# The state stage of an RWKV branch on one NeuronCore: diagonal blocks gathered from PSUM under a mask ahead of the masked copies, the output tail deferred by a tile, and the PSUM banks dealt anew

## The reference

```
for each token t:
    S = S * decay_t                       # per key channel
    sa = S . kk_t                         # what the state holds for this key
    S = S - outer(sa, b_t) + outer(v_t, k_t)
    y_t = S . r_t
out = (group_norm(y) * g + b + bonus_t * v_t) * gate_t
```

## Time and profile before

| | us |
|---|---|
| median of 3 runs | 5111.66 (5102.7 to 5111.89) |
| the profiled execution | 5108.83 |
| its span | 5107.0 |
| window 1835 to 2760, which holds the state stage | 925.0 |
| mean granted clock of the whole span | 0.907 |

### The profile page before, as it was taken

One profiled execution on the slowest core, in us unless ns is written; L12 is line 12 of the kernel. 1 busy time (PEld: TensorE's weight loads), 2 busy tenths in 40 slices (PEclk: granted clock), 3 DMA queues, 4 the chain that ended last, 5 costly groups with the idle time before them and its releaser, 6 DMA issues. The chain is left out here.

```text
span 5107.0 us, 67890 instructions
## 1 busy us (share of the span) xinstructions
PE 4415.9 (86%) x24875; PEld 3721.9 (73%) x24932; DVE 2559.9 (50%) x4995; ACT 1321.3 (26%) x2626; POOL 598.2 (12%) x585
## 2 busy tenths in 40 slices
PE   8999688887799958888886999799979799699869
PEld 6777577776577748878885888677868577577657
DVE  4444334444566655554553434577753333467733
ACT  3222222111222211111111111566641211222211
POOL 0000011111000012222221111000000011011100
PEclk9999799999899967777776999799989899899979
DMA  3111311111543321100102222610023422422233
GB/s 132 58 53 50 123 56 56 56 64 38 184 137 129 122 77 38 33 32 29 37 31 89 99 111 103 185 41 28 15 75 133 146 103 97 148 87 89 81 122 115
DMA packets 218306, 434.06 MB, mean 85 GB/s; under 512 B 36547, under 2 KB 90436, under 8 KB 218022
## 3 DMA queue, kind: packets, MB, share of 16 engines
q1 hardware_dynamic: 218150, 432.02, 24.8%
HBM read 248.33 MB, written 146.93 MB: 77 GB/s over the span
## 5 line engine op out<-in xcount | busy, mean ns | idle before, releaser
L235 PE MATMUL rp_pj<-rp_w_high,rp_hT_high 128*128 128x512 f32 (+1 forms) x640 | 239.5, 383 | 27.2 <-DVE rp_w_low L178 14.4
L235 PE MATMUL fp_pj<-fp_w_high,fp_hT_high 128*128 128x512 f32 (+2 forms) x640 | 220.7, 359 | 43.8 <-DVE fp_w_low L178 43.8
L2484 DVE TENSOR_SCALAR_CACHE_REDUCE fa_sm<-fa_sc 128x512 f32<-128x512 f32 (+2 forms) x320 | 194.4, 610 | 93.3 <-PE fa_sc L2325 82.9
L236 PE MATMUL rp_pj<-rp_w_low,rp_hT_high 128*128 128x512 f32 (+1 forms) x640 | 233.6, 374 | 0.0
L235 PE MATMUL hg_pj<-hg_w_high,hg_hT_high 128*128 128x512 f32 x512 | 210.1, 410 | 17.1 <-DVE hg_w_low L178 17.1
L235 PE MATMUL rc_pj<-rc_w_high,rc_hT_high 128*128 128x512 f32 (+1 forms) x512 | 192.6, 384 | 34.5 <-DVE rc_w_low L178 34.4
L236 PE MATMUL fp_pj<-fp_w_low,fp_hT_high 128*128 128x512 f32 (+2 forms) x640 | 219.2, 357 | 0.0
L1527 PE MATMUL rw_b<-rw_U_parts_high,rw_pick_row 128*128 128x128 f32 x256 | 106.4, 416 | 116.3 <-DVE rw_U_parts_low L178 116.3
L236 PE MATMUL hg_pj<-hg_w_low,hg_hT_high 128*128 128x512 f32 x512 | 205.1, 400 | 0.0
L2339 PE MATMUL fa_tp<-fa_ident,fa_sm 128*128 128x128 f32 x1088 | 175.1, 282 | 31.4 <-DVE fa_pT_low L178 14.8
L2432 ACT CAST fa_pT_high<-fa_tp 128x512 fp32r<-128x512 f32 (+1 forms) x288 | 160.9, 559 | 147.5 <-PE fa_tp L2339 145.3
(11 more groups left out here) (552 smaller groups left out, 11634.2 us busy)
## 6 DMA issues: line engine op xcount, KB each, us to landing
rw_given<-rw_packed_dram SPq DMA_DIRECT2D x48, 512.0 KB, 4.2
rc_back<-rc_XB SPq DMA_DIRECT2D x48, 336.0 KB
rw_packed_dram<-rp_M SPq DMA_DIRECT2D x48, 256.0 KB, 2.6
rp_M<-rp_U SPq DMA_DIRECT2D x16, 728.0 KB, 4.8
hg_xt<-in_x SPq DMA_DIRECT2D x16, 512.0 KB, 3.7
kept_x_high_dram<-hg_hT_high SPq DMA_DIRECT2D x16, 512.0 KB, 3.5
kept_x_low_dram<-hg_hT_low SPq DMA_DIRECT2D x16, 512.0 KB, 4.3
sw_hT_high<-kept_x_high_dram SPq DMA_DIRECT2D x16, 512.0 KB, 3.7
```

Of the source, the lines that this page charges most:

```text
L235: pe.matmul(out, hT.high[:, kc, :], self.high[:, kc, lo:hi], start=kc == 0, stop=False)
L236: pe.matmul(out, hT.high[:, kc, :], self.low[:, kc, lo:hi], start=False, stop=False)
L2484: dve.tensor_scalar(sm[:, to:to + cols], bank_of(slot)[:, 0:cols], 0.0, NEG, ALU.add, ALU.max, accum_out=tops[:, four, c:c + 1]).then_inc( ...
```

## The change

Five things change, all in `rwkv`:
1. `compact_blocks` no longer reads `BA` from SBUF with four operations over 32 partitions each. It multiplies the four PSUM products with a mask `near` (own 16x16 block, above the diagonal) into `X`, sums the eight blocks with one reduction into `Uc`, and comes ahead of all masked copies.
2. The spread is cut in two halves on other banks (6, 7, then 2, 3), and the last group of products (n = 1, r = 1) goes between the halves, into banks 0 and 1, after the first two copies of `BA`.
3. The solve waits for six masked copies instead of eight; the read-out waits for all eight. Banks: Z 4, y 5, state product 1. The wait for the renewed state moves from the transposes to level 4.
4. The third part of `finish` becomes `put_out` and is done one tile later, after the state is renewed; `y`, `gain` and `rest` get a second buffer, and the store follows a step later. Parts 0 and 1 stand ahead of levels 5 and 6, which is where they stood.
5. POOL makes the two corners of level 4 first, each behind its two copies of `BA`, and `gain` and `rest` after them. The decay of the state on DVE moves behind the masked copies of `BA` and two of `KA`.

```diff
-        Y_BANK, Z_BANK, INC_BANK = 5, 6, 7
+        Z_BANK, Y_BANK, INC_BANK = 4, 5, 1
+        SPREAD = (6, 7, 2, 3)
-        PRODUCT_BANKS = (((0, 1), (2, 3)), ((4, 5), (6, 7)))
+        PRODUCT_BANKS = (((0, 1), (2, 3)), ((4, 5), (0, 1)))
...
@@ PE
-                    for n in range(2):
-                        for r in range(2):
-                            multiply(i, pi, n, r)
-                    spread(i)
+                    multiply(i, pi, 0, 0)
+                    multiply(i, pi, 0, 1)
+                    multiply(i, pi, 1, 0)
+                    spread(i, 0)
+                    pe.wait_ge(masked, 8 * i + 2)
+                    multiply(i, pi, 1, 1)
+                    pe.wait_ge(masked, 8 * i + 4)
+                    spread(i, 1)
                 if m:
                     if pr:
-                        pe.wait_ge(masked, 8 * i + 8)
+                        pe.wait_ge(masked, 8 * i + 6)
                     solve(t, pt)
-                    read_out(t, pt)
+                    read_out(t, pt, i)
...
@@ DVE
-            def compact_blocks(i, pi):
-
+            def compact_blocks(i):
+
+                for r in range(2):
+                    dve.wait_ge(products, 4 * i + r + 1)
+                    for o in range(2):
+                        tt(X[:, 4 * r + o:4 * r + 4:2, :], heads(B[PRODUCT_BANKS[0][r][o]][:], 2)[:, :, 0:P], again(near[:], 2), ALU.mult)
+                dve.drain()
+                dve.tensor_reduce(Uc[:], X[:].rearrange("p h (b t) -> p h t b", t=SMALL), AX, ALU.add)
+                dve.drain()
+                dve.tensor_copy(Up.high[:], Uc[:])
+                dve.drain()
+                Up.take_low(dve, lambda ap: ap[:], Uc[:]).then_inc(parts_ready, 1)
                 dve.tensor_copy(Ys[:], own_rows[:])
-                for q in range(P // (2 * SMALL)):
-                    rows_, at = slice(2 * SMALL * q, 2 * SMALL * (q + 1)), 2 * SMALL * q
-                    dve.scalar_tensor_tensor(Uc[rows_], BA[pi][rows_, :, 0, at + SMALL:at + 2 * SMALL], odd_block[rows_, :], BA[pi][rows_, :, 0, at:at + SMALL], ALU.mult, ALU.add)
...
             def step(i, hi, pi, t, ht, pt):
                 pr, m = i is not None, t is not None
+                last = m and not (isinstance(t, int) and t == 0)
+                if pr:
+                    compact_blocks(i)
+                    for r in range(2):
+                        mask_products(i, pi, 0, r)
+                    mask_products(i, pi, 1, 0)
                 if m:
                     dve.wait_ge(vg_here[pt], 48 * (ht + 1))
                     decay(pt, 0).then_inc(S_in, 1)
                 if pr:
-                    for r in range(2):
-                        mask_products(i, pi, 0, r)
-                    dve.drain()
-                    compact_blocks(i, pi)
-                    for r in range(2):
-                        mask_products(i, pi, 1, r)
+                    mask_products(i, pi, 1, 1)
+                    dve.drain()
+                if pr:
                     invert_blocks(i, pi)
-                    dve.drain()
+                dve.drain()
                 if m:
                     renew_state(t, pt)
+                if last:
+                    put_out(t - 1, 1 - pt)
```

More of the change, by code:

```diff
@@ L1421, in rwkv @@
         inc, tmp = sb("inc", [P, RW]), sb("tmp", [P, RW])
-        gain, rest = sb("gain", [P, RW]), sb("rest", [P, RW])
+        gain, rest = ([sb(f"{n}{p}", [P, RW]) for p in range(2)] for n in ("gain", "rest"))
         S = sb("S", [P, PAIRS, P])
@@ L1498, in turn_two @@
                 if two == 0 and t is not None:
+                    pe.wait_ge(SA_ready, t + 1)
                     pe.wait_ge(y_ready, t + 1)
-                if two == 1 and t is not None:
-                    pe.wait_ge(SA_ready, t + 1)
-                    pe.wait_ge(inc_taken, t + 1)
                 for name, bank in TURNED[2 * two:2 * two + 2]:
@@ L1553, in level @@
                     pe.wait_ge(T1_ready, done + g + 1)
+                    if l == FIRST and g == 0 and t is not None:
+                        pe.wait_ge(inc_taken, t + 1)
                     if l > FIRST:
@@ L1653, in step @@
                     act.wait_ge(y_done, t + 1)
-                    act.copy(y[:], B[Y_BANK][:]).then_inc(y_ready, 1)
+                    if not (isinstance(t, int) and t < 2):
+                        act.wait_ge(out_ready, t - 1)
+                    act.copy(y[pt][:], B[Y_BANK][:]).then_inc(y_ready, 1)
                 if pr:
@@ L1677, in step, with corner @@
                 pr, m = i is not None, t is not None
-                if m:
[L1679 to L1685, removed]
+                def corner(l, g):
+                    if l > FIRST:
+                        pool.wait_ge(T1_done, PER_TILE * i + 2 * (l - FIRST) + g - 1)
+                    pool.tensor_tensor(CT[:, 4 * g:4 * g + 4, :], BA[pi][:, 4 * g:4 * g + 4, 0, :], again(blocks[:, l - FIRST, :], 4), ALU.mult).then_inc(CT_ready, 1)
@@ new lines, in step @@
+                if pr:
+                    for g in range(2):
+                        pool.wait_ge(masked, 8 * i + 2 * g + 2)
+                        corner(FIRST, g)
+                if m:
+                    pool.wait_ge(vg_here[pt], 48 * (ht + 1))
+                    if not (isinstance(t, int) and t < 2):
+                        pool.wait_ge(out_ready, t - 1)
+                    pool.tensor_tensor(gain[pt][:], given_of(pt, "gate"), gn_g[:], ALU.mult)
+                    pool.tensor_tensor(heads(rest[pt][:], RW_HEADS), heads(given_of(pt, "v"), RW_HEADS), spread(bonus[pt][:], RW_DIM), ALU.mult)
```

82 lines of the change are left out of this document (43 added, 39 removed).

## The result

| us | before | after |
|---|---|---|
| median (runs) | 5110.2 (4, 5102.7 to 5111.89) | 5077.83 (4, 5073.13 to 5092.28) |
| profiled execution, its span | 5108.83, 5107.0 | 5092.28, 5090.5 |
| 15 full steps of the stage | 836.76 | 816.73 |

The ratio is 0.9944, with a 95% interval of 0.9922 to 0.9967: faster by 32 us, where 165 were forecast. 4946 and the range from 4885 to 5030 both missed. The profiled execution of the changed kernel is the slowest of its four, so the 20 us that the table shows for the stage are those of that execution. Lines L... are now those of the changed kernel, and in the experiments those of each run's own kernel. "PE", "DVE", "ACT" and "POOL" are the engines as named above; a *tile's length* is the distance from its first product to that of the next tile. There are 15 such distances; the first is that of tile 0, which is only prepared.

A forecast was written before the change was run, and what follows sets the result against it. The state stage was taken as a chain where PE waits for DVE and its clock then falls. 0.6 × 15 + 0.4 × 5.5 = 11.2 us a step, times 15 = 168, less 5: 163, so 4946 us; range 4885 to 5030.

The forecast's parts named there:

- Gather: DVE's masked products and reduction at the tile's start: parts ready at 4.9 us instead of 11.4; reduction 1.22.
- PE: PE's wait before the spread shrinks from 7.7 to 2.2 us; the fourth product group is now on the path.
- POOL beside it: `gain` and `rest` beside the inversion's first 4 us hold up DVE: 2.0 us lost, `XT` at 23.3.
- Output tail: Three output operations moved behind the state renewal: nothing charged, up to 1 us on some tiles.
- Tile, clock kept: Tile at full clock, PE waiting for `XT` until 23.4 us: 40.7 against the mean of 55.8, 15 us less.
- How often it falls: Share of tiles losing PE's clock at a 2.2 us gap: a straight line gives 0.46, taken as 0.4.
- the prediction's own signs of being wrong: A clock of 0.50 throughout spread and solve in every tile, a reduction of several us, or a late level 4 correction.
- The other reading offered: Thin work counts against PE's clock: a 0.67 us gap between narrow matmuls of SA and y made it fall.
- the clock would have been kept, 4884 us: Rival in which PE's clock never falls: 15 × 15 = 225 us gained, 4884 us; chance 0.13.
- Tile, clock fallen: Tile with PE's clock fallen: 31.7 us against 37.3 up to the first turn, 5.5 us less.
- rival 1: PE's clock falls in every tile: 15 × 5.5 = 83 us gained, 5026 us; chance 0.14.

The follow-up runs named there:

- experiment 3: Changed kernel with the masked product written in the order of summing, so the reduction reads neighbours, in eight smaller products: 5066.4 us, 0.9922.
- experiment 5: Changed kernel with six useless matmuls in PE's gap and POOL's `gain` and `rest` back ahead of the first two corners: 4877.92 us, 0.9548.
- experiment 4: Changed kernel with POOL's `gain` and `rest` back ahead of the first two corners: 5017.38 us, 0.9817.
- experiment 10: Changed kernel with the third part of the output back behind level 6 and eleven useless matmuls in PE's gap: 4920.0 us, 0.9622.
- experiment 12: Changed kernel with the old gather behind the copies of `BA` and 16 useless matmuls in PE's gap: 4948.33 us, 0.9683.
- experiment 2: Kernel before the change with thirteen useless matmuls in PE's wait ahead of the spread: 4985.21 us, 0.975.
- experiment 1: Changed kernel with six useless matmuls in PE's gap ahead of the spread: 4887.4 us, 0.956.
- experiment 6: Changed kernel with three useless matmuls in PE's gap: 4885.36 us, 0.956.
- best: Changed kernel with three useless matmuls in PE's gap, POOL's old order and the reduction over neighbours: 4897.62 us, 0.9583.
- experiment 8: Also written `after_pad`: changed kernel, gap left open, with three useless matmuls on PE's path behind the level 4 transposes: 5041.08 us, 0.9863.
- experiment 9: Changed kernel, gap left open, with six useless matmuls on PE's path behind the level 4 transposes: 5077.44 us, 0.9929.
- experiment 11: Changed kernel with the old gather behind the copies of `BA` and nine useless matmuls in PE's gap: 5112.22 us, 0.9997.

## Why the prediction was wrong

**"Gather": right in kind, mis-sized.** Parts at 5.45 us instead of 4.9; the reduction 1.86 instead of 1.22, which experiment 3 puts on the stride. The prediction charged nothing for it by an operation of 8 elements, too short to show it. By the Trainium skill (SBUF — State Buffer, Door 1: The DMA port swizzle), crossing to a new 16-byte line costs extra; the run agrees, with 0.64 us for 1024 elements.

**"PE": right.** The wait is 2.6, forecast 2.2; the fourth product group takes 2.08 us at half clock, forecast 1.8.

**"POOL beside it": right in kind, and near in size at full clock**: 1.8 us on the first three pairs (experiment 5), forecast 2.0; with the clock fallen it is 1.0 on the first two (experiment 4), off PE's path. Of the 1.8 PE's wait for `XT` shows 1.1.

**"Output tail": no loss, as said.** With the new gather its place is worth 1 to 2 us a tile (experiment 10). The parts are not worth anything singly: with the old gather, all the other moves together give a tile of 44.6 at full clock, where the old kernel has 44.3 (experiments 12 and 2). There the gathers stand beside POOL's operations and take 5.17 instead of 4.14 us, the cast 1.26 instead of 0.23; that this eats what the earlier place has won is my reading, no run parts the two.

**"Tile, clock kept": right**, 40.7 and 40.68 (experiment 1), though not to the last digit: the prediction's own terms, 23.4 + 17.8 − 0.7, give 40.5. PE was ready for the first turn at 22.1 us (forecast 21.2) and `XT` came at 23.2 (forecast 23.4).

**"How often it falls" failed first.** A straight line between gaps of 0.5 and 4.2 us gave 0.4 of the tiles at 2.2 us. The runs show a much steeper passage. Behind tile 0, no tile lost the clock for more than 7 us at 0.7 to 1.1 us (experiments 12 and 6), three did at up to 1.3 (`best`; three more in experiment 2), ten at 2.0, and at 2.6 every one in the change and all but one in experiment 3. That the clock stayed low throughout spread and solve in every tile was one of the prediction's own signs of being wrong. The two ends of the line were too far apart to carry a straight line between them: nothing in the trace of before lay between 0.7 and 4.2 us. The other reading offered, that thin work between the gaps brings the fall, does not hold as it stands: the same narrow matmuls, with the same pause of 0.7 us before y, ran at 1.00 as soon as the gap was closed. The Trainium skill (TensorE: Matmul & The Clock Gate, Why this matters for your kernels) warns only of longer gaps than this one. By that rule the clock would have been kept, 4884 us, and the measurement decides against it.

**"Tile, clock fallen" failed too, and rival 1 with it.** Rival 1 had the right condition (a fall in every tile) and the wrong price: 5.5 us a tile, 83 in all, against 20 in the stage of the profiled execution. The step assumed that the low clock ends at the same piece of work as in rows 4, so that what is saved ahead of it is saved in the tile. It lasted longer: the whole read-out and the start of the turn ran at 0.50. A tile came to 54.6 instead of 50.3. By the 0.41 us of experiments 8 and 9, 50.3 would need some 23 us at the low level; measured are 33.9. That is the mis-sized term. The kernel before had 29 us of it a step on average (0.74 of 836.76 over 15) and the changed one 33.8 (0.69 of 816.73), and this accounts for the small gain: 3.6 us less at full clock, 0.41 × 4.8 = 2.0 back, an estimate of 1.6 against the 1.3 measured.

What sets the 33.9 us is shown only in part. Shown: the fall comes at one place in each tile (some 5.1 us behind the first product, within the gap), lengths repeat exactly, and the low time is not fixed by the length of the gap: it was 0 in one tile of experiment 3 and mostly 20 to 24 us in `after_pad`, at the same 2.6 us, and 17 us in experiment 4 at 2.8. My reading is that the fall and the tiles lock together: a tile that comes late to its gap does less work at the high clock before the next change of level, and vice versa, until a length repeats. That reading is argued; it names no length in advance, and it did not foresee that `after_pad` would be the faster. Why POOL's order (experiment 4) lands at 17 us and 47.7 stays open.

## What to carry to other kernels

Price a shorter wait at both clock levels, and find out first how long the new kernel spends at each: here the change is worth 3.6 us a tile at full clock and 1.3 where it falls (836.76 − 816.73 over 15), and a clock that is held throughout is worth 11.5 in the old kernel (55.8 to 44.3) and 13.8 in the new (54.5 to 40.7). The filled runs gave less, 125 and 190 us over the program, 8 and 13 a tile, since the clock still fell in some of their tiles. Where PE waits some 2 us in every pass of a loop, a kernel with a few useless matmuls in the gap belongs beside every other experiment; without it a small edit can show some 40 to 60 us that belong to the clock.

## What the runs showed that was not expected

- Three fillers, 1.3 us of work that nobody needs, took 192 us off the program (5077.83 to 4885.36).
- A microsecond at the low level lengthened a tile by some 0.41 us, in the change and in both padded kernels.
- With the same gap of 2.6 us one tile of experiment 3 kept the clock and took 40.7 us, its neighbours 53.2 and 54.6.
- Behind a gap of 2.6 us PE stayed at 0.50 for some 34 us, through work without a pause of over 0.7 us; the same work ran at 1.00 with the gap closed. A tile of the kernel before had as much (33.8 us), which rows 4 do not show.
- A reduction whose neighbours lie 64 bytes apart takes 1.86 us for 1024 elements against 1.22 side by side; the eight smaller products that write it so cost 0.36 us each against four of 0.42, so nothing is won.
- A cast of 128 elements that takes 0.23 us alone took 1.26 beside POOL operations (experiment 11).
- Adding work to PE's path made the program 37 us faster (experiment 8).
